# A decoder trunk kernel: x transposed ahead of its norm and kept by channel, the residual added by VectorE, two input blocks kept in SBUF

## The chip, the cores and the metric

The kernel runs on one core of one Trainium2 chip. Its engines are TensorE (PE: matmuls, and PEld: weight loads), VectorE (DVE), ScalarE (ACT), GpSimd (POOL) and SyncE (SP), which here issues all DMAs from one queue, in program order. The metric is the device time of one execution in microseconds (us), lower is better. Time before: 2696.9 us, the median of 3 runs (2691.5 to 2698.01).

## The reference

One layer of a hybrid decoder, on 2048 prompt tokens and 32 sampled ones (8 sequences of 4), width 1024:

```python
u = rmsnorm(h, norm_mix_g);  proj = u @ w_in            # 2824 columns: q, k, v of A and C, z, x/B/C, dt
oa = banded_attention(qa, ka, va, 128, 1, tab_a, sinks)  # A: 4 q heads, 2 kv heads, key distance 0..128
oc = sum over (128,1), (512,4), (2048,16) of dilated_banded_attention(qc, kc, vc, window, dil)  # weighted per query
ob = rmsnorm(ssd_chunked(silu(conv(xbc)), dt, A, B, C) + d_skip * xs, gated by silu(z)) * ssm_norm_g
h = h + concat(oa, ob, oc) @ w_out                       # the residual that the change touches
h = h + square(relu(rmsnorm(h, norm_mlp_g) @ w_up)) @ w_down
```

`rmsnorm(x, g)` is `x * rsqrt(mean(x*x) + 1e-6) * g`. Matrices are float32. Outputs are h of all tokens, the keys and values, and the scan's and the convolution's states. The sampled tokens run the same formulas against caches.

## The kernel before, in words

Every large product is made of three fp16 matmuls (high by high, high by low, low by high): a float32 operand is split into a high fp16 half and the rest, by ACT (high) and DVE (low). A product of 128 output channels by 512 tokens over 1024 input channels is 24 matmuls.

Two stages follow each other, with a barrier between them.

**Tokens stage** (`tokens`, lines 92 to 620). `plan()` yields units in one order, and each engine walks through that list and does its part of each unit. Tokens go in five blocks: 512, then the 32 sampled ones, then three of 512. For each block: `load_x` (L234) reads x by token, `rms` on ACT (L353) takes squares and the inverse root, `norm` on DVE (L452, instruction at L456) scales x by it in place, `turn` transposes one slab of 128 channels on PE (L547, L555) into one of two PSUM banks, ACT writes the high half `u` (L372), DVE the low half (L462). PE's next turn but one waits for that low half, since it frees the bank. The weights are split meanwhile (`split_w`, L394 and L467). `pair` (L567) multiplies the first two tiles of 128 tokens while the last weights come; a unit "prod" is a third of the columns of one tile (24 matmuls; L564), taken by ACT (L382), with sums and scales by head on DVE (`head_sums`, `head_scale`) and gains on POOL (L342, L343). Once per tile a "z" unit splits one slab of the remaining weights (L401 on ACT, L492 on DVE), and PE uses it after the next tile's first third. `store_u` writes both halves of every block of 512 to DRAM.

**Core stage** (`core`, lines 650 to 2567), in four blocks of 512 tokens (the last one has 544, in pieces of 256 and 288). First "col" units: convolution and gate channels from `pu`, the halves of the normed input, which `load_pu` (L1130) reads back from DRAM (blocks 0 and 1 at the start, 2 and 3 as slots come free), with attention and scan units between them. Then per block "out" (w_out, the residual), "sum" (the norm), and four rounds of 8 "up" and 8 "down". In the last round a down unit of block b, the transposed store "y" of the channel before, and an out unit of block b+1 alternate. Weights come through a ring of 5 slots (`fetch`, L1110); in block 0 they come raw and are split (L1530, L1779) and kept in DRAM.

"out" before: PE first puts x into the bank, transposed, as float32 matmuls against the identity times 64 (`out`, L2218 to L2232; L2229), then adds the 24 matmuls (L2204 is the helper's line for all of those). ACT copies the bank to `h` (L1573) and squares it (L1583), which frees the bank; POOL sums the squares (L1507). "sum" is a matmul with ones (L2238), ACT's Ln and Exp (L1589, L1592), and then for 8 slabs DVE's product (L1792), ACT's high half (L1595), DVE's low half (L1788).

## Time and profile before

| | |
|---|---|
| median of 3 runs | 2696.9 us |
| the profiled execution's own time | 2695.12 us |
| its span | 2693.2 us |
| PE busy | 2476.5 us (92%) |
| DVE, ACT, POOL busy | 1194.0, 843.8, 278.5 us |
| mean granted TensorE clock | 0.962 of full speed |
| DMA moved | 414.33 MB |

The tokens stage runs from 0 to about 328 us, the core stage from there to the end. A line of a timeline is an instruction or a run of like ones; "x8" counts records (one float32 matmul is two records), and the bracket tells how long the engine had been idle before it and what ended that. SPq is the queue on which SP issues DMAs. DMA "to landing" is from issue to completion.

### The profile page before, as it was taken

To read this page: it belongs to the slowest core of one execution; us is meant where nothing else is said; L and a number is where in the kernel's file an instruction comes from. 1 tells how busy PE (TensorE), PEld (TensorE's weight loads), DVE (VectorE), ACT (ScalarE), POOL (GpSimd) and SP (SyncE) were. 2 spreads that over 40 slices of the span, in tenths; PEclk is the share of its full clock that TensorE was granted. 3 is DMA by queue.
4 is the path that set the end of the run, shared out by engine and by line. 5 is a ranking of instruction groups with operands and counts; after the bars stand their busy time and mean duration, and the time that the engine had idled before them with its cause. 6 is when DMAs were issued, how large, how long until landed. Compare 5 with 4: busy or idle time off the path is not lost.

```text
span 2693.2 us, 43459 instructions
## 1 busy us (share of the span) xinstructions
PE 2476.5 (92%) x17747; PEld 1459.6 (54%) x17747; DVE 1194.0 (44%) x2780; ACT 843.8 (31%) x1528; POOL 278.5 (10%) x306
## 2 busy tenths in 40 slices
PE   7799679798878999999899999897999999899999
PEld 4355336354434555544455554443655446688887
DVE  4245345466634767752354564105556620322222
ACT  4332244265343543431243331114342211301110
POOL 0011213011101211000111110011201000000000
PEclk9899888899999999999999999998999999999999
DMA  6335373455554566776434465433445544222222
GB/s 220 120 115 183 135 236 127 161 188 165 171 185 158 197 199 212 252 235 211 127 110 138 146 175 155 152 125 96 156 154 169 163 150 124 79 95 95 95 95 85
DMA packets 342822, 414.33 MB, mean 154 GB/s; under 512 B 60704, under 2 KB 271520, under 8 KB 342369
## 3 DMA queue, kind: packets, MB, share of 16 engines
q1 hardware_dynamic: 342624, 411.55, 47.5%
q8 instruction: 142, 2.33, 0.4%
q14 instruction: 56, 0.45, 0.1%
HBM read 304.19 MB, written 107.30 MB: 153 GB/s over the span
## 4 chain that ended last, share of the span: by engine, by line
PE 71%; DVE 6%; ACT 3%; issue 3%; DMA 2%; SPq 2%; POOL 0%; POOLq 0%; DVEq 0%; ACTq 0%
PE core_dense L2204 60%; PE core_spare L2309 2%; PE core_spare L2323 1%; PE core_dense L2229 1%; PE core_spare L2335 1%; PE core_spare L2297 1%; PE core_spare L2458 1%; DVE core_col L1921 1%; DMA core_js<-scratch_sums 1%; DVE core_h L1815 1%; DMA core_ring<-scratch_kept_w 1%; DVE core_r L1792 1%; PE core_spare L2438 1%; DVE core_p L1847 0%; ACT core_p L1638 0%
## 5 line engine op out<-in xcount | busy, mean ns | idle before, releaser
L2204 PE MATMUL core_dense<-core_u,core_ring 128*128 128x512 f16 (+2 forms) x4800 | 884.1, 344 | 26.2 <-DVE core_u L1788 17.7
L2204 PEld LDWEIGHTS core_dense<-core_u,core_ring 128*128 128x128 f16 x4800 | 472.0, 99 | 404.0 <-issue 46.2
L2204 PE MATMUL core_dense<-core_r_hi,core_ring 128*128 128x512 f16 (+2 forms) x2560 | 651.4, 340 | 2.5 <-DVE core_h L1815 2.5
L2204 PE MATMUL core_dense<-core_r_lo,core_ring 128*128 128x512 f16 (+2 forms) x1280 | 435.4, 340 | 0.0
L2204 PEld LDWEIGHTS core_dense<-core_r_hi,core_ring 128*128 128x128 f16 x2560 | 251.0, 98 | 198.6 <-issue 7.6
L2204 PE MATMUL core_dense<-core_pu,core_ring 128*128 128x512 f16 x1152 | 272.2, 394 | 30.1 <-DMA core_pu<-scratch_u 22.5
L1815 DVE SCALAR_TENSOR_TENSOR core_h<-core_dense,core_h 128x512 f32<-128x512 f32 (+2 forms) x160 | 94.3, 590 | 424.9 <-PE core_dense L2204 424.6
L1603 ACT ACTIVATE core_r<-core_dense 128x512 f32<-128x512 f32 (+2 forms) x160 | 82.4, 515 | 545.4 <-PE core_dense L2204 545.3
L1803 DVE TENSOR_TENSOR core_r<-core_r 128x512 f32<-128x512 f32 (+2 forms) x160 | 96.9, 605 | 335.4 <-ACT core_r L1603 334.9
L2204 PEld LDWEIGHTS core_dense<-core_pu,core_ring 128*128 128x128 f16 x1152 | 115.6, 101 | 166.7 <-issue 27.7
L564 PE MATMUL tok_prod<-tok_w_hi,tok_u 128*128 128x512 f16 (+1 forms) x768 | 203.4, 355 | 0.0
L2204 PEld LDWEIGHTS core_dense<-core_r_lo,core_ring 128*128 128x128 f16 x1280 | 125.5, 98 | 93.7 <-issue 1.3
L1779 DVE SCALAR_TENSOR_TENSOR core_ring<-core_staged,core_ring 128x1024 f16<-128x1024 f32 x72 | 90.1, 1253 | 127.6 <-ACT core_ring L1530 126.5
L564 PE MATMUL tok_prod<-tok_w_lo,tok_u 128*128 128x512 f16 (+1 forms) x384 | 135.9, 354 | 0.0
L1638 ACT ACTIVATE core_p<-core_p,core_neg 128x256 f32<-128x256 f32 (+1 forms) x256 | 99.7, 461 | 92.0 <-DVE core_neg L1854 91.4
L1471 POOL TENSOR_TENSOR core_v_hi<-core_qkv,core_ones 128x256 f16<-128x256 f32 (+1 forms) x82 | 62.9, 767 | 524.7 <-DMA core_qkv<-out_tok 273.5
L1921 DVE SCALAR_TENSOR_TENSOR core_col<-core_conv_raw,core_cw,core_col 128x512 f32<-128x512 f32 x96 | 75.5, 786 | 92.6 <-ACT core_conv_raw L1550 90.3
L1507 POOL TENSOR_TENSOR core_ssum<-core_ssum,core_r 128x512 f32<-128x512 f32 (+1 forms) x28 | 35.9, 1283 | 743.6 <-ACT core_r L1583 743.6
L564 PEld LDWEIGHTS tok_prod<-tok_w_hi,tok_u 128*128 128x128 f16 x768 | 75.9, 101 | 67.0 <-issue 7.1
L1806 DVE TENSOR_TENSOR core_r_lo<-core_r,core_r_hi 128x512 f16<-128x512 f32 (+2 forms) x160 | 99.2, 620 | 17.0 <-DVE core_r L1803 0.5
L1847 DVE CUSTOM_DVE_ANT_0 core_p<-core_spare,core_bias 128x256 f32<-128x256 f32 (+1 forms) x256 | 81.2, 372 | 31.4 <-PE core_spare L2323 28.9
L1573 ACT ACTIVATE core_h<-core_dense 128x512 f32<-128x512 f32 (+2 forms) x40 | 20.7, 517 | 221.6 <-PE core_dense L2204 217.2
(299 smaller groups left out, 2736.8 us busy)
## 6 DMA issues: line engine op xcount, KB each, us to landing
core_ring<-scratch_kept_w SPq DMA_DIRECT2D x264, 512.0 KB, 4.3
scratch_kept_w<-core_ring SPq DMA_DIRECT2D x72, 512.0 KB, 5.6
core_qkv<-out_tok SPq DMA_DIRECT2D x48, 384.0 KB, 5.7
core_staged<-in_w_up SPq DMA_DIRECT2D x32, 512.0 KB, 4.7
core_staged<-in_w_down SPq DMA_DIRECT2D x32, 512.0 KB, 5.1
out_tok<-tok_tok SPq DMA_DIRECT2D x16, 644.0 KB, 3.0
core_piece<-in_c_kt SPq DMA_DIRECT2D x32, 288.0 KB, 4.0
core_piece<-in_c_v SPq DMA_DIRECT2D x16, 576.0 KB, 4.5
```

The lines of the kernel that those rows point to most:

```text
L564: last = pe.matmul(bank[0:nt, 0:w], l, r[:, k, c0:c0 + w], start=k == 0 and i == 0, stop=k == KT - 1 and i == 2, skip_group_check=True)
L1471: pool.tensor_tensor(hi, v, ones[:, 0:w].rearrange("p (h d) -> p h d", d=HD), ALU.mult).then_inc(vh_ready, 1)
L1603: act.activation(r[:, n % 2, 0:w], bank_of["up", b, f, q][:, 0:w], ACT.Relu, scale=1.0 / (WS * HS)).then_inc(r_ready, 1)
L1638: last = act.activation(p[:, hh, cols], p[:, hh, cols], ACT.Exp, bias=neg[:, hh:hh + 1])
L1779: dve.scalar_tensor_tensor(ring[:, q % R, :, 1, :], w_raw[n % RW], WS, ring[:, q % R, :, 0, :], ALU.mult, ALU.subtract).then_inc(lo_split, 1)
L1803: dve.tensor_tensor(r2[:, n % 2, 0:w], r[:, n % 2, 0:w], r[:, n % 2, 0:w], ALU.mult).then_inc(r2_ready, 1)
L1806: dve.tensor_tensor(r_lo[:, f % HF, off:off + w], r2[:, n % 2, 0:w], r_hi[:, f % HF, off:off + w], ALU.subtract).then_inc(rl_ready, 1)
L1815: dve.scalar_tensor_tensor(here, bank_of["down", b, i, q][:, 0:w], HS * HS / WS, here, ALU.mult, ALU.add).then_inc(down_added, 1)
L1847: last = dve.tensor_tensor_reduce(p[:, hh, cols], spare[1 + bank][:, :].rearrange("p (a c) -> p a c", c=2 * P)[:, at, cols], bias[:, BIAS_ ...
L1921: dve.scalar_tensor_tensor(dst, conv_raw[:, i, j:j + 512], cw[:, i, j:j + 1], dst, ALU.mult, ALU.add).then_inc(tap, 1)
L2204: ins = pe.matmul(bank, w[:, k, part, :], s, start=first and j == 0, stop=last and j == 2, skip_group_check=True)
L2309: last = pe.transpose(spare[3 + b][:, at:at + P], p[:, 2 * b + hh, half * P:(half + 1) * P], ident[:, :])
```

## The change

In the tokens stage the order of the blocks of rows becomes 1024, sampled, 1536, 0, 512. PE transposes x as it was read. ACT copies the bank to `xs` (float32, two buffers), which frees the bank; SP stores `xs` to a new DRAM array `xt`, by channel, and a buffer is written again only when its store has landed. A new unit "spread" puts the token's inverse roots into all partitions (four float32 matmuls of `rr` against the identity on PE, copied to `rb` by ACT). DVE then makes `un` = xs * gain * rb, ACT the high half from it, DVE the low half one turn later. DVE's `norm` by token is gone. The sums of squares of the second and third block are made earlier, and `store_tok` comes two thirds of a tile later. Only the first two blocks of 512 are stored by `store_u`; the last two stay in SBUF, in the place where the core stage has `pu`, and `load_pu(0)` and `load_pu(1)` are gone.

In the core stage PE no longer adds x. SP loads x by channel from `xt` (one DMA a unit), and DVE makes `h` = bank / 64 + x, which frees the bank. ACT squares `h`.

```diff
-        BLOCKS = ((0, 4, P), (SEQ, 1, NS), (512, 4, P), (1024, 4, P), (1536, 4, P))
+        BLOCKS = ((1024, 4, P), (SEQ, 1, NS), (1536, 4, P), (0, 4, P), (512, 4, P))
...
+            yield "spread", 0, 0, 0
...
-            todo = [("rms", 1, 0, 0)] + [("turn", 1, k, 0) for k in range(KT)] + [("rms", 2, 0, 0)] + [("turn", 2, k, 0) for k in range(KT)] + [("rms", 3, 0, 0)]
+            todo = [("rms", 1, 0, 0), ("rms", 2, 0, 0), None, ("spread", 1, 0, 0)] + [("turn", 1, k, 0) for k in range(KT)]
+            todo += [("spread", 2, 0, 0)] + [("turn", 2, k, 0) for k in range(KT)] + [("rms", 3, 0, 0)]
...
-                todo = [("turn", n + 1, k, 0) for k in range(KT)] if n + 1 < NBK else []
+                todo = [("spread", n + 1, 0, 0)] + [("turn", n + 1, k, 0) for k in range(KT)] if n + 1 < NBK else []
...
+        def turned_free(eng, kind, n, k):
+
+            i = turned_no[kind, n, k] - NTURN
+            if i >= 0:
+                was, m, j = turned_as[i]
+                if was == "spread":
+                    eng.wait_ge(rb_ready, m + 1)
+                else:
+                    eng.wait_ge(xs_ready, turn_no[m, j] + 1)
...
+                def store_x(n, k):
+                    i = turn_no[n, k]
+                    s, w = BLOCKS[n][0], BLOCKS[n][1] * BLOCKS[n][2]
+                    sp.wait_ge(xs_ready, i + 1)
+                    sp.dma_start(io["xt"][:, k, s:s + w], xs[:, i % 2, 0:w]).then_inc(xs_out[i % 2], 16)
...
                     act.wait_ge(turn_done, i + 1)
+                    if i >= 2:
+                        act.wait_ge(xs_out[i % 2], 16 * (i // 2))
+                    act.activation(xs[:, i % 2, 0:w], turned[turned_no["turn", n, k] % NTURN][:, 0:w], ACT.Copy).then_inc(xs_ready, 1)
                     if n != SMP and u_no[n] >= 2 and k == 0:
                         act.wait_ge(u_out[u_no[n] % 2], 32)
-                    act.activation(u_of(n, 0, k, w), turned[i % NTURN][:, 0:w], ACT.Copy, scale=g_mix[:, k:k + 1]).then_inc(uh_ready, 1)
+                    act.wait_ge(un_ready, i + 1)
+                    act.activation(u_of(n, 0, k, w), un[:, i % 2, 0:w], ACT.Copy).then_inc(uh_ready, 1)
+
+                def give_factors(n):
+                    w = BLOCKS[n][1] * BLOCKS[n][2]
+                    act.wait_ge(spread_done, n + 1)
+                    if n:
+                        act.wait_ge(un_ready, turn_no[n - 1, KT - 1] + 1)
+                    act.activation(rb[:, 0:w], turned[turned_no["spread", n, 0] % NTURN][:, 0:w], ACT.Copy).then_inc(rb_ready, 1)
...
-                def norm(n):
-                    _, tiles, nt = BLOCKS[n]
-                    dve.wait_ge(rms_ready, n + 1)
-                    for j in range(tiles):
-                        dve.tensor_scalar(x[0:nt, n % 2, j, :], x[0:nt, n % 2, j, :], rr[0:nt, n % 2, j:j + 1], None, ALU.mult).then_inc(normed, 1)
+                def low(n, k):
+                    i = turn_no[n, k]
+                    w = BLOCKS[n][1] * BLOCKS[n][2]
+                    dve.wait_ge(uh_ready, i + 1)
+                    dve.tensor_tensor(u_of(n, 1, k, w), un[:, i % 2, 0:w], u_of(n, 0, k, w), ALU.subtract).then_inc(ul_ready, 1)
 
                 def turn(n, k):
                     i = turn_no[n, k]
                     w = BLOCKS[n][1] * BLOCKS[n][2]
-                    dve.wait_ge(uh_ready, i + 1)
-                    dve.scalar_tensor_tensor(u_of(n, 1, k, w), turned[i % NTURN][:, 0:w], g_mix[:, k:k + 1], u_of(n, 0, k, w),
-                                             ALU.mult, ALU.subtract).then_inc(ul_ready, 1)
+                    dve.wait_ge(xs_ready, i + 1)
+                    dve.wait_ge(rb_ready, n + 1)
+                    if i >= 2:
+                        dve.wait_ge(ul_ready, i - 1)
+                    dve.scalar_tensor_tensor(un[:, i % 2, 0:w], xs[:, i % 2, 0:w], g_mix[:, k:k + 1], rb[:, 0:w],
+                                             ALU.mult, ALU.mult).then_inc(un_ready, 1)
+                    if k:
+                        low(n, k - 1)
+                    if k == KT - 1:
+                        low(n, k)
...
-                    if i >= NTURN:
-                        pe.wait_ge(ul_ready, i - NTURN + 1)
+                    turned_free(pe, "turn", n, k)
                     for j in range(tiles):
                         if k == 0:
-                            pe.wait_ge(normed, tiles_before[n] + j + 1)
-                        last = pe.transpose(turned[i % NTURN][:, j * nt:(j + 1) * nt], x[0:nt, n % 2, j, k * P:(k + 1) * P], ident[0:nt, 0:nt])
+                            pe.wait_ge(x_in[n % 2][j], x_loads(n, j))
+                        last = pe.transpose(turned[turned_no["turn", n, k] % NTURN][:, j * nt:(j + 1) * nt], x[0:nt, n % 2, j, k * P:(k + 1) * P], ident[0:nt, 0:nt])
                     last.then_inc(turn_done, 1)
+
+                def spread_factors(n):
+                    _, tiles, nt = BLOCKS[n]
+                    turned_free(pe, "spread", n, 0)
+                    pe.wait_ge(rms_ready, n + 1)
+                    for j in range(tiles):
+                        last = pe.matmul(turned[turned_no["spread", n, 0] % NTURN][:, j * nt:(j + 1) * nt], rr[0:nt, n % 2, j:j + 1].to_broadcast([nt, P]),
+                                         ident[0:nt, 0:nt], start=True, stop=True)
+                    last.then_inc(spread_done, 1)
...
+            pu = before.left
...
-                        sp.wait_ge(out_done, order["out", bb, ii, len(PIECES[bb]) - 1] + 1)
+                        sp.wait_ge(out_added, order["out", bb, ii, len(PIECES[bb]) - 1] + 1)
                     s, w = start(b), width(b)
-                    cols = slice(i * P, (i + 1) * P)
-                    sp.dma_start(x[:, n % XR, 0:4, :], io["x"][s:s + 512, cols].rearrange("(t p) c -> p t c", p=P)).then_inc(x_in[n % XR], 16)
-                    if w > 512:
-                        sp.dma_start(x[0:w - 512, n % XR, 4, :], io["x"][s + 512:s + w, cols]).then_inc(x_in[n % XR], 16)
+                    sp.dma_start(x[:, n % XR, 0:w], io["xt"][:, i, s:s + w]).then_inc(x_in[n % XR], 16)
 
...
-                load_pu(0)
...
-                load_pu(1)
...
-                        bank = bank_of["out", b, i, q]
-                        act.wait_ge(out_done, n + 1)
-                        if b:
-                            act.wait_ge(y_done, y_no["y", b - 1, i])
-                        if b == i == 0:
-                            act.wait_ge(conv_done, KT * 4)
-                            for j in range(2):
-                                act.wait_ge(col_out[j], 16 * 6)
-                        act.activation(h[:, i, off:off + w], bank[:, 0:w], ACT.Copy, scale=1.0 / WS)
+                        act.wait_ge(out_added, n + 1)
...
-                        act.activation(dst[:, off:off + w], bank[:, 0:w], ACT.Square, scale=1.0 / WS).then_inc(out_sq, 1)
+                        act.activation(dst[:, off:off + w], h[:, i, off:off + w], ACT.Square).then_inc(out_sq, 1)
...
+                def out(b, i):
+                    for q, off, w in pieces(b):
+                        n = order["out", b, i, q]
+                        if b:
+                            dve.wait_ge(y_done, y_no["y", b - 1, i])
+                        if b == i == 0:
+                            dve.wait_ge(conv_done, KT * 4)
+                            for j in range(2):
+                                dve.wait_ge(col_out[j], 16 * 6)
+                        dve.wait_ge(x_in[(KT * b + i) % XR], 16 * ((KT * b + i) // XR + 1))
+                        dve.wait_ge(out_done, n + 1)
+                        dve.scalar_tensor_tensor(h[:, i, off:off + w], bank_of["out", b, i, q][:, 0:w], 1.0 / WS, x[:, (KT * b + i) % XR, off:off + w],
+                                                 ALU.mult, ALU.add).then_inc(out_added, 1)
...
-                    n = KT * b + i
-                    here = [KT * bb + ii for bb in range(b + 1) for ii in range(KT) if KT * bb + ii <= n and (KT * bb + ii) % XR == n % XR]
-                    pe.wait_ge(x_in[n % XR], 16 * sum(2 if j // KT == NB - 1 else 1 for j in here))
                     w_s = weights("out", b, i)
                     for q, off, w in pieces(b):
                         bank = begin("out", b, i, q)
-                        for j, (t, at, rows) in enumerate(tiles(b, off, w)):
-                            pe.matmul(bank[:, at:at + rows], x[0:rows, n % XR, t, :], ident_w[0:rows, 0:rows], start=j == 0, stop=False, skip_group_check=True)
                         for kk in range(KT):
-                            last = thrice(bank[:, 0:w], w_s, kk, u[:, 0, kk, off:off + w], u[:, 1, kk, off:off + w], False, kk == KT - 1)
+                            last = thrice(bank[:, 0:w], w_s, kk, u[:, 0, kk, off:off + w], u[:, 1, kk, off:off + w], kk == 0, kk == KT - 1)
```

How the instructions move is shown at three places. The first is ACT at the start of the tokens stage, from the inverse root (`tok_rr`) to the second slab of weights; before:

```order
L364 ACTIVATE tok_rr<-tok_ss 128x4
L372 ACTIVATE tok_u<-tok_turned,tok_g_mix 128x512 x2
L394 ACTIVATE tok_w_hi<-tok_w_raw 128x1288
L372 ACTIVATE tok_u<-tok_turned,tok_g_mix 128x512 x2
L394 ACTIVATE tok_w_hi<-tok_w_raw 128x1288
```

And of the change, where `tok_rb` is the spread factors, `tok_xs` the copy by channel and `tok_un` the normed product that DVE makes between two ACT instructions:

```order
L404 ACTIVATE tok_rr<-tok_ss 128x4
L423 ACTIVATE tok_rb<-tok_turned 128x512
L412 ACTIVATE tok_xs<-tok_turned 128x512
L416 ACTIVATE tok_u<-tok_un 128x512
L412 ACTIVATE tok_xs<-tok_turned 128x512
L416 ACTIVATE tok_u<-tok_un 128x512
L445 ACTIVATE tok_w_hi<-tok_w_raw 128x1288
```

What was one ACT instruction a turn is two, and the second stands behind DVE's product of the same turn.

The second is PE in the last round of a block of the core stage, between the transposed store of one channel (`core_ident,core_h`) and the next down unit (`core_r_hi`); before:

```order
L2275 MATMUL core_dense<-core_ident,core_h 128x128 x4
L2229 MATMUL core_dense<-core_ident_w,core_x 128x128 x4
L2204 MATMUL core_dense<-core_u,core_ring 128x512 x24
L2204 MATMUL core_dense<-core_r_hi,core_ring 128x512
L2204 MATMUL core_dense<-core_r_lo,core_ring 128x512
```

And of the change:

```order
L2337 MATMUL core_dense<-core_ident,core_h 128x128 x4
L2271 MATMUL core_dense<-core_u,core_ring 128x512 x24
L2271 MATMUL core_dense<-core_r_hi,core_ring 128x512
L2271 MATMUL core_dense<-core_r_lo,core_ring 128x512
```

The four matmuls of x are gone from each of those units; nothing else moves on PE there.

The third is SP at the start of the core stage, from the first ring slot to the next; before:

```order
L1123 DMA core_ring<-scratch_kept_w 128x2048
L1134 DMA core_pu<-scratch_u 128x8x512 x2
L1370 DMA core_ident<-in_ident 128x128
L1195 DMA core_qkv<-out_tok 128x768
...
L1185 DMA core_bias<-scratch_lines 128x4x256 x2
L1134 DMA core_pu<-scratch_u 128x8x512 x2
L1123 DMA core_ring<-scratch_kept_w 128x2048 x3
```

And of the change:

```order
L1189 DMA core_ring<-scratch_kept_w 128x2048
L1432 DMA core_ident<-in_ident 128x128
L1258 DMA core_qkv<-out_tok 128x768
...
L1248 DMA core_bias<-scratch_lines 128x4x256 x2
L1189 DMA core_ring<-scratch_kept_w 128x2048 x3
```

The four DMAs of `core_pu` are gone and the rest stands in the same order.

## Rows read from the trace of the kernel before

**Rows 1.** The page's first line.
```profile
span 2693.2 us, 43459 instructions
```
**Rows 2.** PE's waits: line, released by, us in total, times, longest.
```profile
PE core_dense L2204 <- DMA core_pu<-scratch_u: 22.5, 1, 22.5
...
PE tok_turned L555 <- DVE tok_x L456: 17.6, 7, 6.9
PE core_dense L2204 <- DMA core_ring<-scratch_kept_w: 15.8, 2, 8.3
...
PE tok_turned L555 <- DVE tok_u L462: 7.9, 5, 3.9
...
PE tok_turned L555 <- DVE tok_u_s L462: 4.7, 2, 4.0
```
**Rows 3.** Line L2229's records: shortest/median/longest ns, first and last start.
```profile
L2229 PE MATMUL core_dense<-core_ident_w,core_x x272: 271/275/552, 794.7 to 2309.7; 128*128 128x128 f32 x128, 32*128 32x32 f32 x8
```
**Rows 4.** Timeline of PE, block 0's out units: start, us, then what.
```profile
808.34 1.05 PE L2229 MATMUL core_dense<-core_ident_w,core_x 128*128 128x128 f32 x8
809.23 5.34 PE L2204 MATMUL core_dense<-core_u,core_ring 128*128 128x512 f16 x24
```
**Rows 5.** Timeline of PE and SP, start of the core stage.
```profile
328.10 0.33 SPq L1123 DMA_DIRECT2D core_ring<-scratch_kept_w  x1
...
339.99 7.14 PE L2204 MATMUL core_dense<-core_pu,core_ring 128*128 128x512 f16 x24 [22.53 <-DMA core_pu<-scratch_u]
...
350.95 5.54 SPq L1123 DMA_DIRECT2D core_ring<-scratch_kept_w  x3
...
362.88 5.04 PE L2204 MATMUL core_dense<-core_pu,core_ring 128*128 128x512 f16 x12 [7.54 <-DMA core_ring<-scratch_kept_w]
```
**Rows 6.** Timeline, start of the tokens stage.
```profile
19.75 0.20 ACT L364 ACTIVATE tok_rr<-tok_ss 128x4 f32<-128x4 f32 x1
...
20.96 1.05 PE L555 MATMUL tok_turned<-tok_ident,tok_x 128*128 128x128 f32 x2 [6.86 <-DVE tok_x L456]
...
24.81 1.27 ACT L394 ACTIVATE tok_w_hi<-tok_w_raw 128x1288 f16<-128x1288 f32 x1
...
32.81 1.06 PE L564 MATMUL tok_prod<-tok_w_hi,tok_u 128*128 128x512 f16 x2
```
**Rows 7.** Timeline of a norm in the core stage.
```profile
844.96 0.60 ACT L1573 ACTIVATE core_h<-core_dense 128x512 f32<-128x512 f32 x1 [4.04 <-PE core_dense L2204]
...
850.04 1.41 DVE L1792 SCALAR_TENSOR_TENSOR core_r<-core_h,core_g,core_rs 128x512 f32<-128x512 f32 x2 [7.64 <-ACT core_rs L1592]
850.83 1.29 ACT L1595 ACTIVATE core_u<-core_r 128x512 f16<-128x512 f32 x2 [0.82 <-DVE core_r L1792]
```
**Rows 8.** Timeline of PE, turns of the second and third block.
```profile
69.21 0.28 PE L555 MATMUL tok_turned<-tok_ident,tok_x 32*128 32x32 f32 x2 [3.14 <-DVE tok_x L456]
...
121.11 0.66 PE L555 MATMUL tok_turned<-tok_ident,tok_x 128*128 128x128 f32 x4 [1.13 <-DVE tok_u L462]
```
**Rows 9.** Stretches: us, busy (and count) by engine, PEclk, DMA share, GB/s.
```profile
62.00:100.00 38.00, 22.95 (x102) 10.98 (x100) 11.19 (x23) 11.27 (x30) 4.43 (x4) 0.84 0.24 91
100.00:150.00 50.00, 44.83 (x228) 24.88 (x229) 19.08 (x29) 15.93 (x33) 4.43 (x4) 0.88 0.32 111
```
**Rows 10.** Timeline of DVE, per-head sums (first row) and scales (second) of a tile.
```profile
109.23 0.56 DVE L476 TENSOR_TENSOR tok_sq<-tok_tok 128x384 f32<-128x384 f32 x1 [5.76 <-ACT tok_tok L382]
...
111.43 1.15 DVE L487 TENSOR_TENSOR tok_tok<-tok_tok,tok_hrr 128x384 f32<-128x384 f32 x2
```
**Rows 11.** Records of two lines, ns as in rows 3.
```profile
L492 DVE SCALAR_TENSOR_TENSOR tok_z_w<-tok_z_raw,tok_z_w x12: 1215/2064/2125, 152.7 to 314.5; 128x1024 f16<-128x1024 f32 x12
...
L343 POOL TENSOR_TENSOR tok_tok<-tok_tok,tok_g_head x17: 1259/1267/2251, 66.4 to 321.0; 128x512 f32<-128x512 f32 x16, 32x512 f32<-32x512 f32 x1
```
**Rows 12.** Stores of a tile in the tokens stage: count, KB each, us to landing.
```profile
out_tok<-tok_tok SPq DMA_DIRECT2D x15, 644.0 KB, 3.0
```
**Rows 13.** DMAs of x in the core stage, shortest/median/longest us to landing.
```profile
DMA to landing us min/median/max: 2.5/3.2/11.6
```

123 lines of the change are left out of this document (71 added, 52 removed).

## The prediction

> **What bounds the kernel now.** I read the page first: PE is busy 92% of a span of 2693.2 us [rows 1]. So time goes only where PE loses work or a wait. Then PE's waits [rows 2]: the longest single one, 22.5 us, is the start of the core stage, for `pu` from DRAM; another wait there is for a ring slot (15.8 us in two). The tokens stage waits 17.6 us for the normed x and 7.9 + 4.7 us for the low halves that free a PSUM bank. Then the records of the line that adds x [rows 3], and the timelines of the four places where the change acts [rows 4 to 8]: in each the reader is to see what ends PE's idle time, and what ACT, DVE and SP did ahead of it.
>
> **The change, part by part.** The profiled execution took 2695.1 us, 1.9 over its span and 1.8 under the median of the runs; I sum against 2695.1 and add 1.8.
>
> *The residual leaves PE.* 272 records go [rows 3]. Eight of them take 0.89 us from start to start of what follows (809.23 less 808.34) [rows 4], so 272 / 8 x 0.89 = 30.3 us, all on PE's own path, as the bank and the weights are there. What could eat it: DVE now adds (about 0.7 us) and must do so before ACT squares. The bank is free after one pass and not two (0.60 us each on ACT [rows 7]), which is sooner; at the end of a block the chain add, square, POOL sum has a hand-over more, some 0.25 us in four blocks. I count these as 0. In block 0 ACT, DVE and SP also split raw weights, once in 6.07 us; the loop add 0.7, square 0.6, high half about 1.1, low half 1.2 to 1.5 is 4.1 us and stays under the 5.2 us that 24 matmuls leave. If it did not, one block in four would lose its 7 us. Term: -30, bounds -22 and -31.
>
> *Core stage, start.* Before, PE begins at 340.0, when the first 2 MB of `pu` have landed; the next stop is at 355.3, until the third ring slot lands at 362.9, issued at 350.95 behind the second 2 MB [rows 5]. Now the first matmul needs only ring slot 0, issued at 328.1: with 4.5 us to land PE starts at 332.6. PE had 15.3 us of work and short waits between 340.0 and 355.3, so it reaches the third slot at 347.9. SP, without four large DMAs ahead, issues that slot by 340 to 345, so it lands at 345 to 350. PE goes on at 348 to 351 and not 362.9: 12 to 15 us. The half-speed matmuls after the long wait (5.04 us for 12, against half of 5.34 for 24 [rows 4, 5]) may go too, 2.4 us. Term: -15, bounds -5 (SP's 22 us of issuing between the two slots stay as they are) and -18.
>
> *Tokens stage, start.* The inverse roots are there at 19.95 and the transposes began at 20.96 behind DVE's scaling [rows 6]. Now PE first spreads the factors (8 records, at the low clock about 1.9 us) and turns the first slab until 23.7, about as before. But the loop a turn is longer: ACT copies (0.6), DVE multiplies (0.75), ACT makes the high half (0.65), and only then takes the next copy. The norm of the core stage has that hand-over: DVE at 850.04, ACT at 850.83, 0.79 us [rows 7]. That is 2.05 us a turn. Two turns and a weight slab (1.27 us on ACT [rows 6], and DVE's 1.5 us for its low half ahead of the next product) come to 6.2 us, where before they took 2.7 to 3.4. PE's last turn needs the copy of turn 5, made at about 39; the first product starts at about 40.5 and not 32.8 [rows 6]. Weights are no limit then. Term: +8, bounds +4 and +14 (each copy also waits for the store of two turns earlier; at 6 us a landing it would add about 1 us to each of three pairs, and the weights queue behind those stores).
>
> *Tokens stage, second and third block.* Here the change gives. From 66.1 (69.21 less 3.14) to 134.9 (121.11, the turn 0.66, and 13.1 us of the sampled block's thirds) are 68.8 us [rows 8]. PE's work in it is 8 thirds, 5 of 5.2 us and 3 of 2.7, and 5.2 us of turns: 39.3. Waits: 17.6 less the 6.9 at the start and 0.7 of small ones, 7.9 less 2.9 in the first block, and 4.7, together 19.7 [rows 2, 6]. The other 9.8 us go with the clock: granted 0.84 and 0.88 in these stretches [rows 9], that is, part of the time at 1.2 GHz after PE had stood still. Now the squares of both blocks are made beforehand, and a bank is free at ACT's copy. New waits: the two sets of squares keep ACT 6.6 us, so the first spread bank is taken 2.9 us late; each third with per-head sums holds DVE 3.3 us (109.23 to 112.5 [rows 10]) ahead of the products, which makes the third turn behind it wait 1 to 2 us, four times. About 9 us in all, and 4.5 of clock by the same proportion, with 40 of work: 53.5. Term: -15, bounds -22 and -8.
>
> *Tokens stage, the rest.* Before, PE does not wait between 135 and 313. Now a tile with a turn in its second and last third runs: take 0.6, sums and scale 3.3, product, high half (5.4), take, copy, product, high half (7.8), z's high half about 1.0 (1.27 for 1288 columns), z's low half 1.2 alone [rows 6, 10, 11]: 10.1 us, and PE wants it at 8.9. Four such tiles at 0.1 to 1.2 us, one tile with squares in its second third 1.3, and two spreads 1.0: +5. Bounds +1 and +14. DVE's product and its low half read two SBUF tiles each; POOL's gains run right behind the same scale. Where such a pair met before, both grew: the z split from 1.22 to 2.06 us and POOL's from 1.26 to 2.25 [rows 11]. If each of four tiles pays one POOL instruction (1.27), that is 5 us more; I have taken 1.5 of it in the 5. The Trainium skill says so too (SBUF — State Buffer, Who interferes with whom): a DVE instruction with two SBUF inputs contends with a GpSimd instruction that reads SBUF, and the loser blocks for the whole instruction; the trace agrees, with the 2.06 and 2.25 just named. By it alone the sum below would be 2654, without it 2649.
>
> Sum: -30 - 15 + 8 - 15 + 5 = -47, thus 2648, and with 1.8 **2650 us**. I allow 2 us for stores sharing the queue with loads: **2652**.
>
> **The rivals.**
> *A: the stores of x set the tokens stage's pace.* Each copy waits for the store two turns back, so two turns take a landing and 1 us. A tile's store of 644 KB lands in 3.0 us [rows 12], which speaks against it; for it, SP issues in order, and stores stand behind waits for POOL and for the z split. At 6 us: 3 pairs at the start +2.4, the 7 pairs of the next blocks 49 in place of 38.6 us, +13 in all; with the port and the upper bounds of the late tiles +22: 2674. The Trainium skill would clear it (DMA: Bandwidth & Descriptors, Anatomy of one DMA): 2.0 us fixed, mostly the write's receipt, and bytes over 436 GB/s, an estimate of 2.6 us for 256 KB.
> *B: the core stage's start does not do what it says.* PE starts at 333, but SP's small DMAs hold the third slot back, and PE stands at the ring until 357: -5 and not -15, 2662. For it: SP's own issuing between slots 0 and 2 took 22.9 us [rows 5]. Against it: part of that is SP blocked behind the 2 MB loads.
> *C: slower than before.* The mechanism of A at a landing of 11.6 us, the longest that a 256 KB load of x took [rows 13]: pairs of 12.6 us; start 3 x 6.4, next blocks 7 x 12.6 - 38.6 = 49.6, later 8 pairs of turns 8 x 3.3: +95, 2747. It decides from about 9.3 us a landing, where the gain is used up. Against it: the median of those loads is 3.2 us, and the tokens stage's queue is busy a third of the time [rows 9].
> *D: no new waits.* DVE and ACT keep up in the tokens stage, the start costs 4: 2637.
>
> **How the numbers follow.** Forecast 0.58 (2644 to 2662), A 0.16, B 0.12, C 0.03, D 0.11. The range 2634 to 2672 leaves C, the far half of A and what is under D. A change of 0.3% is about what a measurement of this kernel can tell from none: 8 us, 2689 to 2705. Only C lies above it: slower 0.03. The worse ends of all five terms together are -22 - 5 + 14 - 8 + 14 = -7, that is 2690, just inside: same 0.02, and faster has the rest, 0.95.
>
> **What would show it.** L2229's 272 records gone and out units of 5.2 us in block 0, with no new wait for `core_h` above 1 us; PE's first matmul of the core stage 4 to 5 us after the first ring DMA, and no wait for `core_pu` there; the first product of the tokens stage at 40 to 41; the stretch from the end of the third tile's first third to the fourth block's first product 52 to 55 us; short PE waits behind the z split. Wrong would be: ACT idle for `scratch_xt` stores, a wait for the ring of over 5 us at the third slot, or the first product after 46.

## The result, and the profile after

| | before | after |
|---|---|---|
| median | 2696.9 us (2691.5 to 2698.0, 4 runs) | 2650.0 us (2643.1 to 2650.8, 4 runs) |
| ratio of the runs | | 0.9829, 95% interval 0.9811 to 0.9847 |
| profiled execution's span | 2693.2 us | 2648.7 us |
| PE busy | 2476.5 us | 2451.4 us |
| mean granted TensorE clock | 0.962 | 0.960 |

The forecast was 2652 (2634 to 2672). The sum came out; not all its terms did, and that it came within 2 us is in part luck: +6.0 and +2.5 us stand against -4.3 and -2.4. I followed the difference between the two traces through places that both have. The profiled executions' spans differ by 44.5 us:

| stretch | where it is read | forecast | trace |
|---|---|---|---|
| start of the tokens stage | first product, 32.8 to 38.4 us | +8 | +5.6 |
| first pair of tiles | its end, 60.7 to 65.8 | 0 | -0.5 |
| second and third block | first table product after it, 140.1 to 130.4 | -15 | -14.8 |
| rest of the tokens stage | its last product, 316.7 to 317.9 | +5 | +11.0 |
| core stage, start | third ring slot, 362.9 to 350.2 | -15 | -13.9 |
| core stage to the first out unit | 794.7 to 784.5 | 0 | +2.5 |
| from there to the end | the end of the span | -30 | -34.3 |

PE's waits of the kernel after answer to [rows 2], columns as there:

```profile
PE core_dense L2271 <- DMA core_ring<-scratch_kept_w: 24.1, 3, 14.3
...
PE tok_turned L610 <- ACT tok_xs L412: 12.7, 9, 2.7
...
PE tok_prod L657 <- DVE tok_z_w L550: 10.4, 6, 3.6
...
PE tok_turned L618 <- ACT tok_rr L404: 6.0, 1, 6.0
```

`core_pu` is gone as a releaser. A wait for z that was 3.6 us in one place is 10.4 us in six, and 6.0 us ahead of the first spread took the place of the 6.9 that was the wait for DVE's scaling. Next, the start of the core stage, SP's and PE's timelines, against [rows 5]:

```profile
329.33 0.34 SPq L1189 DMA_DIRECT2D core_ring<-scratch_kept_w  x1
...
343.95 1.63 SPq L1189 DMA_DIRECT2D core_ring<-scratch_kept_w  x3
```
```profile
333.02 7.75 PE L2271 MATMUL core_dense<-tok_u,core_ring 128*128 128x512 f16 x24 [14.34 <-DMA core_ring<-scratch_kept_w]
...
350.19 2.75 PE L2271 MATMUL core_dense<-tok_u,core_ring 128*128 128x512 f16 x12 [1.22 <-DMA core_ring<-scratch_kept_w]
```

PE starts 3.7 us after the first ring DMA, not 11.9. SP issues the third slot 14.6 us after the first, not 22.9, and PE waits 1.2 us for it, not 7.5; the twelve matmuls behind it run at full speed (2.75 us, before 5.04).

The out units of block 0, against [rows 4], on PE, DVE and ACT; PE's row is all eight units in one:

```profile
784.53 43.53 PE L2271 MATMUL core_dense<-core_u,core_ring 128*128 128x512 f16 x192 [7.74 <-DVE core_ring L1830]
...
831.01 1.10 PE L2300 MATMUL core_dense<-core_ssum,core_ones 128*128 128x512 f32 x2 [2.94 <-POOL core_ssum L1566]
```
```profile
796.43 1.23 DVE L1830 SCALAR_TENSOR_TENSOR core_ring<-core_staged,core_ring 128x1024 f16<-128x1024 f32 x1 [1.64 <-ACT core_ring L1589]
797.58 0.68 DVE L1844 SCALAR_TENSOR_TENSOR core_h<-core_dense,core_x 128x512 f32<-128x512 f32 x1
```
```profile
798.29 0.63 ACT L1634 ACTIVATE core_r<-core_h 128x512 f32<-128x512 f32 x1 [1.89 <-DVE core_h L1844]
798.83 1.04 ACT L1589 ACTIVATE core_ring<-core_staged 128x1024 f16<-128x1024 f32 x1
```

192 matmuls in 43.5 us without a gap: the add of 0.68 us and the square of 0.63 us are hidden, and the longer hand-over at a block's end is 0.34 us (PE waits 2.94 for POOL's sum where it waited 2.60).

Last, DVE and POOL in a late tile of the tokens stage, and PE behind them:

```profile
223.87 1.15 DVE L545 TENSOR_TENSOR tok_tok<-tok_tok,tok_hrr 128x384 f32<-128x384 f32 x2
224.94 0.74 DVE L516 SCALAR_TENSOR_TENSOR tok_un<-tok_xs,tok_g_mix,tok_rb 128x512 f32<-128x512 f32 x1
225.60 1.49 DVE L507 TENSOR_TENSOR tok_u<-tok_un,tok_u 128x512 f16<-128x512 f32 x1
227.23 1.54 DVE L516 SCALAR_TENSOR_TENSOR tok_un<-tok_xs,tok_g_mix,tok_rb 128x512 f32<-128x512 f32 x1
228.69 0.68 DVE L507 TENSOR_TENSOR tok_u<-tok_un,tok_u 128x512 f16<-128x512 f32 x1
230.41 1.22 DVE L550 SCALAR_TENSOR_TENSOR tok_z_w<-tok_z_raw,tok_z_w 128x1024 f16<-128x1024 f32 x1 [1.04 <-ACT tok_z_w L452]
```
```profile
225.10 1.44 POOL L382 TENSOR_TENSOR tok_tok<-tok_tok,tok_g_head 128x384 f32<-128x384 f32 x1 [12.79 <-DVE tok_tok L545]
226.51 1.71 POOL L383 TENSOR_TENSOR tok_tok<-tok_tok,tok_g_head 128x512 f32<-128x512 f32 x1
```
```profile
231.78 0.79 PE L657 MATMUL tok_prod<-tok_u_s,tok_z_w 128*128 128x32 f16 x24 [2.02 <-DVE tok_z_w L550]
232.41 1.09 PE L610 MATMUL tok_turned<-tok_ident,tok_x 128*128 128x128 f32 x4
...
250.51 0.75 PE L657 MATMUL tok_prod<-tok_u_s,tok_z_w 128*128 128x32 f16 x24 [2.02 <-DVE tok_z_w L550]
```

The same two forms of DVE instruction take 0.68 or 0.74 us alone and 1.49 or 1.54 us while POOL is at work. z's low half ends at 231.6 and PE has waited 2.02 us for it. From one z product to the next are 18.7 us; without a wait such a tile takes 15.0 (from 219.75 to 234.76 and from 234.76 to 249.77 in the kernel before). 2.0 of the 3.7 are the wait. The rest is PE's clock: four transposes behind the wait take 1.09 us and not 0.60, and the granted clock is 0.57 from 232 to 236 us and 1.00 from there to 250.

### The profile page after: what moved, and what is told of

Read it like the earlier page. It is cut to its first block, busy times and chain, and to the rows that moved or that the text cites. A ratio compares the mean times of both kernels' runs of the same rounds, so it can differ in the third digit from the quotient of the medians.

```text
span 2648.7 us, 43197 instructions
## 1 busy us (share of the span) xinstructions
PE 2451.4 (93%) x17509; PEld 1432.6 (54%) x17509; DVE 1236.5 (47%) x2843; ACT 847.0 (32%) x1533; POOL 282.0 (11%) x305
## 4 chain that ended last, share of the span: by engine, by line
PE 72%; DVE 7%; ACT 3%; issue 2%; DMA 2%; SPq 1%; POOL 0%; POOLq 0%; DVEq 0%; ACTq 0%
PE core_dense L2271 61%; PE core_spare L2371 2%; PE core_spare L2385 1%; PE core_spare L2397 1%; PE core_spare L2359 1%; DVE core_col L1986 1%; PE core_spare L2520 1%; DVE core_h L1880 1%; DVE core_r L1857 1%; PE core_spare L2500 1%; PE core_spare L2514 1%; DVE core_p L1912 1%; PE core_spare L2454 0%; DMA core_js<-scratch_sums 0%; DMA core_qkv<-out_tok 0%
## 5 line engine op out<-in xcount | busy, mean ns | idle before, releaser
L2271 PE MATMUL core_dense<-tok_u,core_ring 128*128 128x512 f16 x1152 | 274.4, 396 | 15.6 <-DMA core_ring<-scratch_kept_w 15.6
L1880 DVE SCALAR_TENSOR_TENSOR core_h<-core_dense,core_h 128x512 f32<-128x512 f32 (+2 forms) x160 | 94.3, 590 | 342.9 <-PE core_dense L2271 342.7
L2271 PEld LDWEIGHTS core_dense<-tok_u,core_ring 128*128 128x128 f16 x1152 | 116.3, 102 | 154.0 <-issue 24.6
L628 PEld LDWEIGHTS tok_prod<-tok_w_hi,tok_u 128*128 128x128 f16 x768 | 75.0, 99 | 65.8 <-issue 6.5
L1656 ACT ACTIVATE core_r_hi<-core_r 128x512 f16<-128x512 f32 (+2 forms) x160 | 88.0, 550 | 5.1
```

Source lines behind the costliest of these rows:

```text
L628: last = pe.matmul(bank[0:nt, 0:w], l, r[:, k, c0:c0 + w], start=k == 0 and i == 0, stop=k == KT - 1 and i == 2, skip_group_check=True)
L1656: act.activation(r_hi[:, f % HF, off:off + w], r[:, n % 2, 0:w], ACT.Square).then_inc(rh_ready, 1)
L1880: dve.scalar_tensor_tensor(here, bank_of["down", b, i, q][:, 0:w], HS * HS / WS, here, ALU.mult, ALU.add).then_inc(down_added, 1)
L2271: ins = pe.matmul(bank, w[:, k, part, :], s, start=first and j == 0, stop=last and j == 2, skip_group_check=True)
```

## The experiments

Unless said otherwise, each is the kernel after with one edit. Times are medians; times within a run are from its trace. A ratio is to runs of the kernel before that were taken at the same time, and their medians were 2696.0, 2694.8 and 2693.3 us in the three series below, where it was 2696.9 beside the kernel after. So a difference between two medians is uncertain by 1 to 4 us. The four runs of the kernel after lie 7.7 us apart, so the total of a single run decides little, and its trace has to.

### The residual put back on PE

```diff
-                    sp.dma_start(x[:, n % XR, 0:w], io["xt"][:, i, s:s + w]).then_inc(x_in[n % XR], 16)
+                    sp.dma_start(x[:, n % XR, 0:4, :], io["x"][s:s + 512, cols].rearrange("(t p) c -> p t c", p=P)).then_inc(x_in[n % XR], 16)
...
+                        for j, (t, at, rows) in enumerate(tiles(b, off, w)):
+                            pe.matmul(bank[:, at:at + rows], x[0:rows, n % XR, t, :], ident_w[0:rows, 0:rows], start=j == 0, stop=False, skip_group_check=True)
```

> The changed kernel with the residual alone put back: SP loads x by token, PE adds it as 272 records against the scaled identity, ACT copies and squares the bank. The tokens stage, the kept blocks and the stores by channel stay. The forecast's step (each group of eight records costs PE 0.89 us and nothing eats it) gives 30 us over the changed kernel's 2650: 2680, and a stretch from the first out unit of block 0 to its norm that is 7.1 us longer than the changed kernel's 46.5 us. Rival: part of the gain between 784 us and the end came from the clock or from the bank that comes free earlier, and the records are only 20 us of it: 2670 or less. Rival on the other side: the DVE add was free and the old form cost more than its records, 2684 or more.

2681.2 us (2676.8 to 2683.1), ratio to the kernel before 0.9951 (0.9934 to 0.9969): 31 us over the kernel after by medians, 33 by the ratios. By the trace block 0's out units up to the norm take 53.2 us (781.86 to 835.07), where after took 46.5: 6.7 us for 64 records, a little under the 7.1 of the step. From there to the norm of the last block the two differ by 22.9 us, in all 29.7 for the 272 records. The traces of before and after differ by 35.2 us in this stretch, 5.6 more than the edit: the same instructions from the first out unit to the last block's norm took 1520.6 us in the trace of before and 1515.0 in this one.

The clock explains both numbers. Take PE's time in the stretch apart into idle time, busy time at half the granted clock, and the rest:

| stretch from the first out unit to the last norm | before | this run | after |
|---|---|---|---|
| time | 1520.6 us | 1515.0 us | 1485.3 us |
| PE idle | 71.2 | 71.2 | 71.4 |
| busy at half clock | 55.0 | 43.5 | 51.1 |
| busy time less half of that: an estimate of the work at full clock | 1421.9 | 1422.1 | 1388.4 |

The same instructions come to the same work within 0.2 us, and half of the 11.5 us between 55.0 and 43.5 is 5.8, which is the 5.6 above. The records are 33.7 us of work, not 30; 3.8 us of that are hidden here, since the trace of after has 7.6 us more at half clock. The forecast's 30 is right in sum and low in its price.

### The kept blocks stored and loaded again

```diff
-                        if n != SMP and u_no[n] < 2:
+                        if n != SMP:
                             store_u(n)
...
                 fetch(0)
+                load_pu(0)
...
                 load_bias(2)
+                load_pu(1)
```

> The changed kernel with the two kept blocks stored and loaded again, at the places in SP's order where the kernel before had them. The forecast's step (start of the core stage) gives back what the trace of the changed kernel shows as gained there, 13.9 us at the third ring slot counted from the first ring DMA: 2664, PE's first product of the stage 12 us after the first ring DMA and the third slot 34 to 35 us after it. Rival B (the small DMAs on SP set the third slot): only some 5 us, 2655, third slot 26 us after the first.

2662.1 us (2658.8 to 2666.4), ratio 0.9886 (0.9864 to 0.9908): 12 us over after by medians, 15 by the ratios. SP's and PE's timelines:

```profile
328.57 0.34 SPq L1189 DMA_DIRECT2D core_ring<-scratch_kept_w  x1
328.96 1.30 SPq L1200 DMA_DIRECT2D tok_u<-scratch_u  x2
...
351.23 3.51 SPq L1189 DMA_DIRECT2D core_ring<-scratch_kept_w  x1
```
```profile
340.02 7.31 PE L2273 MATMUL core_dense<-tok_u,core_ring 128*128 128x512 f16 x24 [22.11 <-DMA tok_u<-scratch_u]
...
363.09 1.44 PE L2273 MATMUL core_dense<-tok_u,core_ring 128*128 128x512 f16 x3 [7.55 <-DMA core_ring<-scratch_kept_w]
```

The third slot is 34.5 us behind the first ring DMA, where before it was 34.8 and after 20.9: 13.7 us at this place. The stretch from there to the first out unit then takes 431.1 us in this trace and 434.3 in the one of after, with 6.8 us less at half clock, so not all of it is seen at the end. Rival B (SP's small DMAs hold the third slot back) falls: in the kernel after they cost 14.6 us of issuing, and PE, from its start at 333.0, has 16 us of work and small waits until it wants the slot.

### POOL's gains cut to one column

```diff
-                    pool.tensor_tensor(tok[0:nt, t % RT, 0:384], tok[0:nt, t % RT, 0:384], g_head[0:nt, 0:6, :]..., ALU.mult)
-                    pool.tensor_tensor(tok[0:nt, t % RT, 512:1024], ...).then_inc(tok_ready, 1)
+                    pool.tensor_tensor(tok[0:nt, t % RT, 0:1], tok[0:nt, t % RT, 0:1], g_head[0:nt, 0, 0:1], ALU.mult).then_inc(tok_ready, 1)
```

> The changed kernel with POOL's gain multiplications of the tokens stage cut to one column (the gains of q and k heads are left out). Two theories for the 11 us that the tokens stage lost between 130 and 250 us. Port: DVE's product and low half read two SBUF tiles and ran beside POOL's gains, 1.49 and 1.54 us in place of 0.68 and 0.75; without the gains both are at 0.7, PE's waits for the z split fall from 10.4 us to 2 or 3, the last z product of the stage starts 6 to 8 us earlier than 317.9. Order: the chain of take, sums, scale, product, high half, copy, product, high half, z is too long by itself; waits of 7 us or more stay and the stage is 0 to 3 us shorter.

One run, 2637.3 us. DVE of the same tile:

```profile
222.68 0.68 DVE L505 TENSOR_TENSOR tok_u<-tok_un,tok_u 128x512 f16<-128x512 f32 x1
224.22 0.75 DVE L514 SCALAR_TENSOR_TENSOR tok_un<-tok_xs,tok_g_mix,tok_rb 128x512 f32<-128x512 f32 x1 [0.86 <-ACT tok_xs L410]
```
```profile
PE tok_prod L655 <- DVE tok_z_w L548: 6.8, 5, 2.8
```

The slow forms are gone, so they are POOL's doing. The last z product comes 7.0 us earlier (310.9), in the range of the port theory; but the waits for z fell only to 6.8 us, not to 2 or 3. The two tiles that waited 2.02 us wait 1.15, and take 16.3 us, not 18.7: over half of what that tile gained is clock. So both theories hold a part: the chain is 1.15 us too long by itself, and POOL adds 0.9. Of the other 6 us of this run 2 lie at the end of the stage (its last store comes sooner, the first ring DMA is at 320.3) and 4 in the core stage, where nothing was changed: up to the first out unit it has 9.2 us less of PE at half clock.

### The squares of the third block: late in the kernel after, early in the kernel before

```diff
-            todo = [("rms", 1, 0, 0), ("rms", 2, 0, 0), None, ("spread", 1, 0, 0)] + [("turn", 1, k, 0) for k in range(KT)]
-            todo += [("spread", 2, 0, 0)] + ...
+            todo = [("rms", 1, 0, 0), None, None, ("spread", 1, 0, 0)] + [("turn", 1, k, 0) for k in range(KT)]
+            todo += [("rms", 2, 0, 0), ("spread", 2, 0, 0)] + ...
```

> The changed kernel with the squares and inverse roots of the third block of rows put back to where the kernel before had them, between the sampled turns and the third block's. Two theories for the 15 us gained from 66 to 135 us. Squares: about half of it is this; PE waits 5 to 7 us ahead of the second spread (at 98 us) and with the clock the first table product of the third block (130.4 us) comes 7 to 9 us later. Copy: the gain is that a bank is free at ACT's copy; then this run loses 0 to 2 us.

And in the kernel before:

```diff
-            todo = [("rms", 1, 0, 0)] + [("turn", 1, k, 0) for k in range(KT)] + [("rms", 2, 0, 0)] + [("turn", 2, ...
+            todo = [("rms", 1, 0, 0), ("rms", 2, 0, 0)] + [("turn", 1, k, 0) for k in range(KT)] + [("turn", 2, ...
```

> The kernel before with one edit: the squares and inverse roots of the third block of rows right behind those of the sampled ones. If the squares are half of what the changed kernel gained from 66 to 135 us, PE's wait of 6.9 us at 98.7 us goes and some clock with it: 7 to 10 us, 2688. If the bank and DVE's low half are the limit, the wait turns into waits for the low half, 0 to 3 us, 2695.

The first: one run, 2652.1 us, the table product behind the third block's turns at 131.65 and not 130.38. The second: 2682.7 us (2680.9 to 2689.6), ratio 0.9963 (0.9950 to 0.9975), and its table product at 129.3, 10.8 us earlier than in the kernel before, with the last product of the stage at 305.8 and not 316.7. PE's timelines of the two at the third block:

```profile
101.31 2.04 PE L618 MATMUL tok_turned<-tok_ident,tok_rr 128*128 128x128 f32 x8 [6.55 <-ACT tok_rr L404]
109.48 0.66 PE L610 MATMUL tok_turned<-tok_ident,tok_x 128*128 128x128 f32 x4 [0.25 <-ACT tok_xs L412]
```
```profile
92.66 0.66 PE L555 MATMUL tok_turned<-tok_ident,tok_x 128*128 128x128 f32 x4 [0.39 <-DVE tok_u_s L462]
103.23 0.66 PE L555 MATMUL tok_turned<-tok_ident,tok_x 128*128 128x128 f32 x4 [3.86 <-DVE tok_u L462]
```

So the 15 us cannot be shared out between squares and copy: each cures most of it by itself. With the copy and late squares the 6.55 us wait stands, but others shrink (3.04 to 0.82 ahead of the sampled turns, 2.26 and 0.47 to 0.25 among the third block's), and 1.3 us are lost in all. With early squares and no copy 10.8 of 14.8 are there. I had the amount and not the cause: this part of the gain needs no transposed x, only an edit of one list.

### DVE reads the bank, ahead of ACT's copy

```diff
-                    dve.wait_ge(xs_ready, i + 1)
+                    dve.wait_ge(turn_done, i + 1)
...
-                    dve.scalar_tensor_tensor(un[:, i % 2, 0:w], xs[:, i % 2, 0:w], ...
+                    dve.scalar_tensor_tensor(un[:, i % 2, 0:w], turned[...][:, 0:w], ...
```

ACT makes the high half first and copies x behind it.

> The changed kernel with one hand-over less: DVE makes the normed product from the PSUM bank, ahead of ACT's copy of x, and ACT takes the high half first and copies x behind it. If the first product of the stage (38.4 us) was held by ACT copy, DVE product, ACT high half in turn (1.94 us each), two turns and a slab now take about 5 us in place of 5.95 and the first product starts at 35.5 to 36.5. In the late tiles the product no longer reads two SBUF tiles: 0.75 and not 1.54 us beside POOL, PE's z waits fall from 10.4 to 5 to 7 us. In all 5 to 8 us: 2643. Rival: the low half is the one that collides and the stage's later waits swallow the start, 2649 to 2651.

2644.7 us (2642.0 to 2649.7), ratio 0.9817 (0.9802 to 0.9831). The total is near the expectation, the start is not: the first product is at 38.95, no earlier. DVE's timeline there, and in the late tile:

```profile
27.21 1.50 DVE L524 SCALAR_TENSOR_TENSOR tok_w_lo<-tok_w_raw,tok_w_hi 128x1288 f16<-128x1288 f32 x1 [1.88 <-ACT tok_w_hi L444]
28.63 0.74 DVE L515 SCALAR_TENSOR_TENSOR tok_un<-tok_turned,tok_g_mix,tok_rb 128x512 f32<-128x512 f32 x1
...
33.19 1.50 DVE L524 SCALAR_TENSOR_TENSOR tok_w_lo<-tok_w_raw,tok_w_hi 128x1288 f16<-128x1288 f32 x1 [1.75 <-ACT tok_w_hi L444]
```
```profile
226.41 1.05 DVE L506 TENSOR_TENSOR tok_u<-tok_un,tok_u 128x512 f16<-128x512 f32 x1
227.59 0.75 DVE L515 SCALAR_TENSOR_TENSOR tok_un<-tok_turned,tok_g_mix,tok_rb 128x512 f32<-128x512 f32 x1
```

Two turns and a slab are 5.98 us, from slab to slab: DVE waits 1.8 us for ACT's high half of the slab, and the next product stands behind it. In the late tile the product from the bank takes 0.75 us beside POOL (POOL's two run from 225.91 to 228.60), the low half, from two SBUF tiles, 1.05. PE's two waits of 2.02 us become 1.27.

### ACT's copy ahead of the high half

In the first block ACT copies the next slab before it takes the high half of this one (`copy_x(n, k + 1)` ahead of the wait for `un_ready`).

> The changed kernel, only ACT's order in the first block changed: the copy of the next slab of x ahead of the high half of this one. ACT then does not sit idle 0.8 to 0.9 us for DVE in each turn, PE gets the bank earlier, and the first product of the tokens stage starts at 36 us or before, 2 to 3 us earlier than 38.4. Rival A (stores of x): the copy must wait for the store two turns back and is no earlier; first product at 38 to 39.

One run, 2652.0 us, first product at 38.28. ACT's waits for the stores of x, which are 3.0 us in four places in the kernel after, are

```profile
ACT tok_xs L413 <- DMA scratch_xt<-tok_xs: 11.4, 5, 3.8
```

The store of turn 2 stands on SP behind a load of weights that waits for a slab of DVE. A copy one turn ahead runs into it. Rival A's mechanism exists, but the kernel after is paced so that it is seen for 3.0 us only.

### The slab's low half behind the product

On top of the run in which DVE reads the bank; a slab's low half is put off to just behind the next turn's product.

```diff
                                              ALU.mult, ALU.mult).then_inc(un_ready, 1)
+                    if late:
+                        split_w(late.pop())
```

> The run before in which DVE reads the bank (2645), with one edit more: DVE makes the low half of a weight slab behind the next turn's product, and not ahead of it. In that run two turns and a slab took 5.99 us, since the product stood behind the slab on DVE and the slab behind ACT's high half. If that order set the start and not ACT's copy of x, the pair of turns now takes about 4.4 us, the first product starts at 34 to 35 us in place of 38.95, and PE ends the stage 4 to 5 us earlier, 2640. Rival (stores): the copy waits for a store that SP issues behind a weight load, the pair stays at 5.5 to 6 us and the first product at 38.

2645.2 us (2643.7 to 2648.2), ratio 0.9822 (0.9809 to 0.9836). The pair takes 5.33 us, and the first product is at 37.6: 1.3 us and not 4 to 5. DVE still has the slab, a low half and a product in a row (27.20 to 30.2) while ACT is idle 2.06 us. Neither expectation was right. The last z product of the stage is at 312.5 and not 315.7, 3.1 us earlier in the trace, but between this run and the one it builds on the medians show no gain.

### z ahead of the turn

```diff
                         yield "prod", n, j, q
+                        if q == 2:
+                            yield "z", 0, c, 0
                         if todo and (j or q):
                             yield todo.pop(0)
...
-                    yield "z", 0, c, 0
```

> The changed kernel, with the z unit ahead of the turn that follows a tile's last third, and not behind it (ACT and DVE then split z before that turn). PE's waits of 0.5 to 2.0 us for z at 166 to 251 us are gone and so is the slower clock behind the two of 2.0 us (18.7 us for the tile from 231.8 in place of 15.0): 9 to 11 us, the z product now at 305.6 starts at 296, 2640. Rival: ACT is then late with the turn and PE waits for the copy of x instead; 0 to 3 us, 2648.

2641.7 us (2640.7 to 2642.8), ratio 0.9808 (0.9795 to 0.9822): 8 us under the kernel after by medians. By the ratios (0.9808 for 0.9829) it is 5.7 us, and their intervals overlap; in the traces the last z product of the stage is 9.1 us earlier (308.8 for 317.9) and the span 7.8 us shorter. DVE and PE at the tile shown above:

```profile
222.41 1.48 DVE L508 TENSOR_TENSOR tok_u<-tok_un,tok_u 128x512 f16<-128x512 f32 x1
224.41 1.69 DVE L551 SCALAR_TENSOR_TENSOR tok_z_w<-tok_z_raw,tok_z_w 128x1024 f16<-128x1024 f32 x1 [0.52 <-ACT tok_z_w L453]
226.03 0.74 DVE L517 SCALAR_TENSOR_TENSOR tok_un<-tok_xs,tok_g_mix,tok_rb 128x512 f32<-128x512 f32 x1
```
```profile
226.40 0.75 PE L658 MATMUL tok_prod<-tok_u_s,tok_z_w 128*128 128x32 f16 x24
227.00 0.64 PE L611 MATMUL tok_turned<-tok_ident,tok_x 128*128 128x128 f32 x4
```

POOL still slows DVE (1.48, 1.69 us), but z's low half now ends 0.3 us before PE wants it. One wait of 1.16 us is left (196.4, the tile in which ACT also takes the squares of the last block), and the tile from 226.4 takes 15.0 us. The z product expected at 296 is at 296.5.

### All together

The three edits above, three buffers for x by channel, and ring slots 1 to 4 ahead of the small loads.

> All together: DVE reads the bank, the slab's low half behind the product, z ahead of the turn, three buffers for x by channel in place of two, and on SP the ring slots 1 to 4 ahead of the small loads at the core stage's start. If the waits are independent: start 4 us, late tiles 10 to 11 us, third ring slot 1 us, and against those some 2 us that the stretch from 66 to 130 us lost when DVE read the bank: 13 to 15 us under the changed kernel, 2636. Rival: the clock or a later wait swallows half of it, 2643.

2640.2 us (2639.5 to 2643.5), ratio 0.9807 (0.9794 to 0.9821). The last z product of the stage is at 308.6, where z ahead alone has 308.8; so the early start was eaten on the way. PE no longer waits for the third ring slot, which was 1.7 us with z ahead alone. What is left against that run, 1.5 us, is within its scatter. The version to take is z ahead alone.

## Why the prediction was right

**The residual.** The step was right in its sum: 29.7 us in the trace of the experiment, 31 by medians. It was right in the waits too: none for `core_h` over 0.5 us, DVE's add in block 0 under cover. Two errors cancel in it. The price of 0.89 us for eight records was read in block 0, where the work at full clock fell by 7.2 us; in the next two blocks it fell by 7.6 and 7.8, and in the last, where a unit has ten records in two pieces, by 11.2, not by the 8.9 of that price. In all that is 33.7, and the clock took some back. In the three traces with the records PE is busy at half clock for 43.5, 45.7 and 55.0 us of the stretch, in the nine without them for 48.0 to 54.0, so the clock can move such a difference by 3.5 us one way and 5.3 the other.

**The start of the core stage.** Right: -13.9 of -15, PE at 3.7 us behind the first ring DMA, the third slot next as written. The kept blocks are worth 12 to 15 us by medians and ratios.

**The start of the tokens stage.** +5.6 of +8, and the first product at 38.4, ahead of the 40 to 41 that was to show it. The turn's hand-over was as worked out (1.93 us from product to product, forecast 2.05; 5.96 us for two turns and a slab, forecast 6.2), but the copy of turn 5 is at 36.85 and not at 39: two such pairs behind that of turn 1, at 24.93. The cause was only half named: undoing the hand-over did not bring the start forward, since the weight slabs between the turns, in order on ACT and DVE, take the time as well.

**Second and third block.** The stretch of the forecast, from the end of the third tile's first third (71.0) to the first product behind the sampled block's (125.1; it is the third block's, though the forecast calls it the fourth's), is 54.1 us where 53.5 was said. It is made of 6.9 us of waits, 5.8 of clock (half of 11.6 us busy at half clock) and 41.4 of work, where 9, 4.5 and 40 were said. The attribution was wrong in part, as the pair of runs on the squares shows: the early squares alone, or the copy alone, bring most of it.

**The rest of the tokens stage.** This term was mis-sized: +11.0, not +5, though inside its bounds. 6.8 of the 11.0 are waits, 1.7 are clock, and 2.5 are more work for PE, of which two spreads are 1.8 (1.0 was said). The chain was right and where it would show too (short waits behind the z split). I let one POOL instruction meet DVE per tile and took 1.5 us for all; in the trace two of DVE's and both of POOL's grow in each such tile. And I gave the wait no clock: 2.0 us of standing cost 1.7 more. The five waits behind z up to 251 us are 6.8 us in all. The rule of the Trainium skill that I weighed there (SBUF — State Buffer, Who interferes with whom) held in the runs as to when: the slow forms are gone without POOL's gains, and gone for the product once it read one SBUF tile only. That the loser stands for a whole instruction (the page says so of DVE's 2-port modes) the traces do not show: in each such meeting both sides grow, DVE's two instructions by 0.8 us each and POOL's two by 0.45 each (0.99 to 1.44, 1.26 to 1.71). By the rule the sum would have been 2654.

**What was not foreseen.** 2.5 us came back between the third ring slot and the first out unit, all of it between 428 and 493 us (415 and 483 after): up to 428 the two are 13.2 us apart, and at the next two waits for DVE 11.9 and 10.2. The same instructions run 13 us apart in the two traces, so the windows to compare are these (columns as in [rows 9]), before first:

```profile
413.00:453.00 40.00, 37.32 (x324) 26.49 (x323) 19.06 (x80) 16.02 (x34) 8.02 (x11) 0.83 0.35 120
```
```profile
400.00:440.00 40.00, 37.19 (x319) 27.58 (x317) 18.84 (x80) 16.02 (x34) 6.25 (x10) 0.79 0.35 120
```

In both traces the granted clock falls to half here, from 439.2 to 452.9 us before and from 423.2 to 440.3 after, 13.7 and 17.1 us. Over the whole stretch PE is busy at half clock for 49.8 us before and 61.4 after, which costs 5.8 us more, and is idle for 2.8 us less; its work at full clock is 342.9 and 342.3 us. So the 2.5 us are clock. In the traces of all twelve kernels the stretch takes 430.7 to 435.5 us with that work the same within 0.6 us, so 2.5 us there say nothing on the change. Why the clock stays low longer in one trace than in another stays open.

**Rivals.** A: ACT's waits for stores are 3.0 us; refuted as the pace, and shown to be near. B: refuted. C: the longest landing of a store of x was 7.1 us, the median 2.8. The Trainium skill (DMA: Bandwidth & Descriptors, Anatomy of one DMA — SWDGE (gpsimd) path) gives the figures behind the estimate of 2.6 us for DMAs that GpSimd issues; SP issues these stores, and it is the 2.8 that decides. D would have needed the z waits away.

## What to carry to other kernels

- Time each term of a sum by landmarks that both traces have. Here two terms were off by 6 and 4 us and the sum by 2.
- Before a difference of some us between two traces is explained, take PE's time apart into idle, busy at half clock and the work at full clock, and compare windows that hold the same instructions, not the same times. Here equal instructions agreed within 0.7 us of work, while the clock moved a stretch by up to 6.5 us.
- Work that PE needs soon goes ahead of work that it needs late, also when both come from one engine's ordered list: swapping two units was worth 6 to 9 us (ratios, medians, traces) and moved one line.
- Before a stall is put down to the structure of a loop, move the one instruction that comes late. Early squares gave the kernel before 10.8 us of the 14.8 that the new structure brought in that stretch.

## What the hardware did that I had not expected

- A wait of 2.02 us of PE was followed by work at half speed (four transposes 1.09 us and not 0.60), and the tile lost 1.7 us more than the wait. In the run where DVE reads the bank the wait there is 1.27 us, the tile takes 16.4 us, and only 0.17 us is lost beside it. The windows from 230 to 252 us show a granted clock of 0.92 and 1.00; in the first trace it is at half from 232.1 to 235.5 us.
- DVE's product from two SBUF tiles took 1.54 us beside POOL, and 0.75 us beside POOL with one of them in PSUM. POOL's own multiplications grew too beside the first.
